# Attention values of two heads side by side in the array's columns, with the weights divided by their sums before they are turned

## The reference, cut to what matters

```python
s = jnp.einsum('bqkgd,bskd->bkgqs', q, k).astype(jnp.float32) * (HEAD_DIM ** -0.5)
p = jax.nn.softmax(s, axis=-1).astype(v.dtype)
return jnp.einsum('bkgqs,bskd->bqkgd', p, v)
```

## Time and profile before

| | us |
|---|---|
| median of three runs | 1839.14 (1838.22 to 1839.6) |
| the profiled execution, its own time | 1839.81 |
| its span, first to last instruction | 1838.0 |
| PE busy | 1762.8 (96%) |
| DVE busy | 1237.6 (67%) |
| ACT busy | 848.0 (46%) |
| POOL busy | 591.6 (32%) |

### The profile page before, as it was taken

How to read it: one execution, slowest core, us unless ns; L and a number is a source line. 1 busy time by engine, 2 the same in 40 slices (tenths; PEclk the granted TensorE clock), 3 DMA queues, 4 the chain that set the end, 5 groups by cost and what they waited for, 6 DMA issues and landing times.

```text
span 1838.0 us, 27537 instructions
## 1 busy us (share of the span) xinstructions
PE 1762.8 (96%) x10200; PEld 1519.2 (83%) x10200; DVE 1237.6 (67%) x2073; ACT 848.0 (46%) x1336; POOL 591.6 (32%) x360
## 2 busy tenths in 40 slices
PE   7978979999999999999999999999999999999998
PEld 7877878777787888888888887888788899989987
DVE  7889765654669587966788885247535665557873
ACT  6654444545224444334444442345453455546654
POOL 4344424211112212321233323224222243525554
PEclk9989999999999999999999999999999999989999
DMA  8545533241224344542345555324222353535553
GB/s 316 211 149 183 183 115 108 65 150 47 58 72 150 105 161 146 175 155 81 126 138 194 184 184 194 87 76 123 85 69 73 94 174 119 171 92 170 182 195 120
DMA packets 71978, 251.80 MB, mean 137 GB/s; under 512 B 7984, under 2 KB 12336, under 8 KB 71216
## 3 DMA queue, kind: packets, MB, share of 16 engines
q1 hardware_dynamic: 66384, 241.74, 40.0%
q10 hardware_dynamic: 5472, 8.39, 1.4%
HBM read 249.05 MB, written 1.05 MB: 136 GB/s over the span
## 4 chain that ended last, share of the span: by engine, by line
PE 67%; DVE 22%; ACT 6%; issue 4%; DMA 1%; ACTq 0%; POOL 0%; DVEq 0%; POOLq 0%
PE bank L643 50%; DVE w_lo L1642 6%; PE bank L774 4%; PE bank L952 4%; DVE mod_w L1697 3%; DVE conv L2509 3%; PE bank L940 2%; PE bank L931 2%; PE bank L1035 2%; DVE probT L1697 1%; ACT w_hi L1122 1%; PE bank L736 1%; PE bank L1024 1%; DVE conv L2516 1%; DVE fT_lo L2518 1%
## 5 line engine op out<-in xcount | busy, mean ns | idle before, releaser
L597 POOL TENSOR_TENSOR w_lo<-w_raw,w_hi 128x512 fp32r<-128x512 f32 x356 | 591.4, 1674 | 1232.2 <-ACT w_hi L1122 1185.0
L1642 DVE TENSOR_TENSOR w_lo<-w_raw,w_hi 128x512 fp32r<-128x512 f32 x356 | 359.2, 1024 | 291.7 <-ACT w_hi L1122 290.7
L1122 ACT ACTIVATE w_hi<-w_raw 128x1024 fp32r<-128x1024 f32 x356 | 367.7, 1053 | 315.3 <-PE bank L643 263.8
L643 PE MATMUL bank<-hT_hi,w_hi 128*128 128x512 f32 (+1 forms) x1280 | 449.6, 351 | 9.7 <-ACT w_hi L1122 3.6
L643 PE MATMUL bank<-hT_hi,w_lo 128*128 128x512 f32 (+1 forms) x1280 | 439.4, 343 | 0.0
L643 PE MATMUL bank<-hT_lo,w_hi 128*128 128x512 f32 (+1 forms) x1280 | 438.9, 343 | 0.0
L643 PEld LDWEIGHTS bank<-hT_hi,w_hi 128*128 128x128 f32 x1280 | 244.5, 191 | 43.9 <-issue 8.0
L643 PEld LDWEIGHTS bank<-hT_hi,w_lo 128*128 128x128 f32 x1280 | 244.0, 191 | 28.3
L643 PEld LDWEIGHTS bank<-hT_lo,w_hi 128*128 128x128 f32 x1280 | 244.5, 191 | 26.9 <-issue 1.0
L1697 DVE SCALAR_TENSOR_TENSOR mod_w<-mod_w,c_rows 128x1024 f32<-128x1024 f32 x96 | 136.6, 1423 | 1.1 <-DMA mod_w<-in_mod_weights 1.1
L643 PE MATMUL bank<-w_hi,hT_hi 128*128 128x512 f32 x272 | 115.5, 425 | 1.9 <-DVE gkT_lo L2219 1.4
(11 more groups left out here) (361 smaller groups left out, 3149.4 us busy)
## 6 DMA issues: line engine op xcount, KB each, us to landing
w_raw<-in_weights SPq DMA_DIRECT2D x356, 512.0 KB, 4.0
mod_w<-in_mod_weights SPq DMA_DIRECT2D x96, 512.0 KB, 3.9
nbias<-in_window_bias ACTq DMA_DIRECT2D x32, 128.0 KB, 2.7
resid_c<-in_ctx ACTq DMA_DIRECT2D x2, 1024.0 KB, 6.4
c_rows<-in_conditions SPq DMA_DIRECT2D x1, 1024.0 KB, 5.7
gatew<-in_gate_weights SPq DMA_DIRECT2D x1, 1024.0 KB, 12.1
decay<-in_decay SPq DMA_DIRECT2D x1, 1024.0 KB, 5.8
out<-resid_x ACTq DMA_DIRECT2D x2, 512.0 KB, 2.6
```

Of the source, the lines that this page charges most:

```text
L597: nc.gpsimd.tensor_tensor(w_lo[:, s, 0, :], w_raw[:, s, 0:COLS], w_hi[:, s, 0, :].bitcast(F32), ALU.subtract).then_inc(lo0_ready, 1)
L643: mm = pe.matmul(held[key][:, oc], st, mv_, start=(opens and k == 0 and t == 0 and i == 0), stop=(closes and k == tiles - 1 and t == 2), s ...
L1122: a.activation(w_hi[:, p % RING].rearrange("p k n -> p (k n)"), w_raw[:, p % RING, :], ACT.Copy).then_inc(hi_ready, 1)
L1642: v.tensor_tensor(w_lo[:, p % RING, 1, :], w_raw[:, p % RING, COLS:KP * COLS], w_hi[:, p % RING, 1, :].bitcast(F32), ALU.subtract).then_in ...
```

## The change

`a_out` takes two heads at once. The values become stationary (128 keys by 64 columns of one head), the turned weights move (128 queries), and the head decides which half of the array's columns and of PSUM's partitions is used. The result comes out with the head dimension on partitions, so that `a_result` goes away and ACT copies bank 7 straight to `y`. The row sums can no longer be applied at the end (queries now lie in the free dimension): DVE multiplies each unit's weights by the reciprocal of its sum in place, between the exponential and the transposes (`scale`, in odd steps, for the pair of the step before). A tile takes eight steps instead of nine, and `prob` has four slots by head. In a step PE now does: scores, then the values of the pair of step s-4, then the transposes of unit s-2.

```diff
     def prob_of(h, t):
-        return (t * AH + h) % 3
-
-    TILE = AH + 1
+        return h % 4
@@ PE
                     def a_turn(h, t):
-                        pe.wait_ge(*exp_done.at((kind, l, h, t)))
+                        pe.wait_ge(*scaled.at((kind, l, h, t)))
...
                     def a_out(h, t):
 
-                        pe.wait_ge(*drained_at((kind, "t", l, h, t)))
+
+                        pe.wait_ge(*drained_at((kind, "t", l, h + 1, t)))
                         if h == 0:
                             take(pe, (kind, "o", l, t), "out")
                         ps = psum((kind, "o", l, t))
                         n = keys(t) // P
-                        g = h // 4 if kind == "ga" else h
                         for j in range(n):
-                            mm = pe.matmul(ps[:, h * HD:(h + 1) * HD], probT[:, h % 2, j * P:(j + 1) * P],
-                                           v_[:, j, g * HD:(g + 1) * HD], start=(j == 0), stop=(j == n - 1))
-                        if h == AH - 1:
+                            for i in range(2):
+                                g = h // 4 if kind == "ga" else h + i
+                                mm = pe.matmul(ps[i * HD:(i + 1) * HD, h // 2 * P:(h // 2 + 1) * P], v_[:, j, g * HD:(g + 1) * HD],
+                                               probT[:, i, j * P:(j + 1) * P], start=(j == 0), stop=(j == n - 1),
+                                               skip_group_check=True)
+                        if h == AH - 2:
                             mm.then_inc(*filled((kind, "o", l, t)))
...
-                    def a_result(t):
-                        pe.wait_ge(*drained_at((kind, "o", l, t)))
-                        ps = take(pe, (kind, "y", l, t), "out")
-                        for j in range(4):
-                            mm = pe.transpose(ps[:, j * P:(j + 1) * P], prob[:, 3, j * P:(j + 1) * P], ident)
-                        mm.then_inc(*filled((kind, "y", l, t)))
-
-                    for s in range(len(q_tts) * TILE + 3):
...
+                    for s in steps_of(q_tts):
+                        if pair(s, q_tts):
+                            a_scores(*pair(s, q_tts))
+                        if pair(s - 4, q_tts):
+                            a_out(*pair(s - 4, q_tts))
                         if unit(s - 2, q_tts):
                             a_turn(*unit(s - 2, q_tts))
@@ ACT
-                        if h >= 3:
-
-                            act.wait_ge(*filled_at((kind, "t", l, h - 3, t)))
+                        if h >= 4:
+                            act.wait_ge(*filled_at((kind, "t", l, h - 4, t)))
...
                     def turned(h, t):
                         if h >= 2:
-                            act.wait_ge(*probT_used.at((kind, l, h - 2, t)))
+                            act.wait_ge(*probT_used.at((kind, l, h // 2 * 2 - 2, t)))
@@ DVE
-                    def divide(t):
...
+                    def scale(h, t):
+
+
+                        dve.wait_ge(*exp_done.at((kind, l, h + 1, t)))
+                        c = 32 + t % 2 * AH + h
+                        v.reciprocal(rs[:, c:c + 2], ss[:, c:c + 2]).then_inc(*W.next())
                         dve.wait_ge(*W.last())
-                        dve.wait_ge(*filled_at(key))
...
+                        for i in range(2):
+                            p_ = prob[:, prob_of(h + i, t), 0:keys(t)]
+                            v.tensor_scalar(p_, p_, rs[:, c + i:c + i + 1], None, ALU.mult)                                .then_inc(*W.tell(scaled, (kind, l, h + i, t)))
...
+                        if pair(s - 1, q_tts):
+                            scale(*pair(s - 1, q_tts))
                         yield
```

More of the change, by code:

```diff
@@ L325, in prob_of, with pair, steps_of @@
     def prob_of(h, t):
-        return (t * AH + h) % 3
-    TILE = AH + 1
+        return h % 4
     def unit(s, tts):
[L333 to L340, removed]
+        i, h = divmod(s, AH)
+        return (h, tts[i]) if s >= 0 and i < len(tts) else None
+    def pair(s, tts):
+        u = unit(s, tts)
+        return u if u and u[0] % 2 == 0 else None
+    def steps_of(tts):
+        return range(len(tts) * AH + 3)
     def V(name, i=0, n=1):
@@ L434, in build @@
     square_ready = Counter("square_ready")
+    scaled = Counter("scaled")
     swapped = Counter("swapped")
@@ L461, in build @@
                lru_ix, lru_mult, lru_y, merged_hi, merged_ready, merged_sum, ml_e, ml_exp, ml_root, ml_ss, ml_w_ready,
-               ml_y, c_ready, neg_max, post_ms, post_root, probT_used, qk_hi, square_ready, swapped, taps_begun, q_ready,
+               ml_y, c_ready, neg_max, post_ms, post_root, probT_used, qk_hi, square_ready, scaled, swapped, taps_begun, q_ready,
                qk_root, qk_ss, resid_ready, ret_hi, ret_root, ret_var, ret_y, root_ready, rows_ready, xT_hi_ready,
@@ L1432, in result @@
                             .then_inc(*A.drain(key))
-                    for s in range(len(q_tts) * TILE + 3):
+                    for s in steps_of(q_tts):
                         if unit(s - 2, q_tts):
                             turned(*unit(s - 2, q_tts))
[L1437 to L1440, removed]
+                        if pair(s - 4, q_tts) and pair(s - 4, q_tts)[0] == AH - 2:
+                            result(pair(s - 4, q_tts)[1])
+                        if pair(s, q_tts):
+                            h, t = pair(s, q_tts)
                             exponential(h, t)
@@ L2175, in maxes @@
                             .then_inc(*W.tell(neg_max, (kind, l, h, t)))
-                    def divide(t):
[L2180 to L2184, removed]
-                        dve.wait_ge(*W.last())
-                        dve.wait_ge(*filled_at(key))
[L2187 to L2195, removed]
+                    def scale(h, t):
+                        dve.wait_ge(*exp_done.at((kind, l, h + 1, t)))
+                        c = 32 + t % 2 * AH + h
+                        v.reciprocal(rs[:, c:c + 2], ss[:, c:c + 2]).then_inc(*W.next())
+                        dve.wait_ge(*W.last())
+                        for i in range(2):
+                            p_ = prob[:, prob_of(h + i, t), 0:keys(t)]
+                            v.tensor_scalar(p_, p_, rs[:, c + i:c + i + 1], None, ALU.mult)                                .then_inc(*W.tell(scaled, (kind, l, h + i, t)))
+                    for s in steps_of(q_tts):
+                        if pair(s, q_tts):
+                            h, t = pair(s, q_tts)
                             maxes(h, t)
                             maxes(h + 1, t)
-                        if tile_end(s - 3, q_tts) is not None:
-                            divide(tile_end(s - 3, q_tts))
+                        if pair(s - 1, q_tts):
+                            scale(*pair(s - 1, q_tts))
                         yield
```

12 lines of the change are left out of this document (3 added, 9 removed).

## The result

The changed kernel takes 1827.96 us (median of four executions, 1822.04 to 1828.88) against 1839.05 (1838.22 to 1839.6) for the kernel before: a ratio of 0.9933, 95% interval 0.9911 to 0.9955. A second set of executions beside the experiments gave 0.9927 (0.9914 to 0.9941). The change makes the kernel about 0.7% faster, 12 to 13 us. Forecast were 34.7 us and a time of 1804.5, with a range up to 1826: the direction is right, the size a third of what was said, and the time is 2 us above the range.

What follows compares the result with a forecast made beforehand. PE was taken to set the pace inside the attentions. Terms: -31.1 (`a_out`) - 5.3 (`a_result`) - 3.3 (end of layer 1's `na`) + 5 (DVE waits) = -34.7 us, giving span 1803.3 and time 1804.5, range 1795 to 1826.

Steps and rivals of the forecast that it cites:

- the column halves work together: In the new `a_out`, instructions go two at a time: 640 x 0.112/2 = 35.8 us instead of 71.7.
- nothing overlaps: Rival on `a_out`: halves do not overlap or a 64-column load costs as much as 128; 1840.3 us, chance 0.09.
- loads stand bare: Rival on `a_out`: 64-column loads do not hide, each instruction costs 0.163 us; 1873 us in all, chance 0.02.
- the old `a_out` was bound by its loads: On PE, old `a_out` cost 0.112 us per instruction for its load, so moving 128 columns instead of 64 is free.
- the size of the saving on PE: `a_out` saves 31.1 us, `a_result`'s transposes 5.3, and the end of layer 1's `na` 3.3.
- the shape change: Values between scores and transposes on PE change the array's shape once more: 0.10 us per pair, 4.8 for 48 pairs.
- the wait of 1.8 at the end: At the end of layer 1's `na`, PE's wait for `divide` before the last `a_result` goes: 1.8 us saved.
- the half clock at the end: After the last `a_result` of layer 1's `na`, PE's stretch at half clock vanishes: 1.5 us saved.
- Cover is missing in three places ... 5 us.: DVE's scaling makes PE wait 2 us at `ga`'s start, 2 in layer 0's `na`, 1 at layer 1's gate rows.
- the half-covered scaling: Rival: in layer 0's 32 pairs each waits most of 1.1 us for DVE, about +20 us; 1819.5 us, chance 0.08.
- A: Experiments' theory: the scaling's place in DVE's queue makes it late, in `na` above all, costing some 23 us of waits.
- B: Experiments' theory: ACT is late, its copy of turned weights standing behind the pair's values and the exponentials behind that copy.

Runs made afterwards that it cites:

- the later version without scaling: Changed kernel with transposes and values one step later in both attentions, and no reciprocal or scaling: 1807.17 us, ratio 0.9821 to the kernel before.
- the later step: Changed kernel with transposes and values one step later: in both attentions 1815.73 us, ratio 0.9862; in `na` alone 1814.43 us, ratio 0.9853.

## Why the prediction was wrong, step by step

**Right: the column halves work together.** Forecast 0.056 us per instruction; measured 0.055, and 0.109 where one half works alone. The rivals in which nothing overlaps (1840.3) and in which loads stand bare (1873) are out. With the latter goes the rule of the Trainium skill on row groups that the prediction weighed (TensorE: Matmul & The Clock Gate, Part 3, The mechanism): both halves use the same rows here and their loads still don't add to the time. The Trainium skill (TensorEngine Tiling (Array Packing), Theoretical Speedup) gives a speedup of up to 2 where a small dimension is at most 64. The traces agree for the 64 columns here: 0.109 us where one half works alone, 0.055 with both. One step on the way is not borne out: that the old `a_out` was bound by its loads. The instructions of one half alone load 64 columns and move 128, and stand as far apart as the old ones, which load 128 and move 64; the rate doesn't tell which of the two it comes from.

**Nearly right: the size of the saving on PE.** (The 1804.5 is the median of before less 34.7; from the stated span of 1803.3 and the 1.8 us that the time lies above it, it would be 1805.1. Nothing hangs on it.) `a_out` was to save 31.1 us. By the rows it is 1.78 - 1.07 = 0.71 for a full pair, 32 of them 23 us, and about 0.26 for each of the 16 pairs with half the keys, 4 us. So 27. The missing 4 us are the shape change: 1.07 less 16 x 0.055 leaves 0.19 per pair where I took 0.10 with 0.16 as the upper end; 48 x 0.09 = 4.3. `a_result` is gone, 5.3, and so is the wait of 1.8 at the end. In sum 34 us of the 38.2 forecast without the clock. The runs confirm the order of it: with the scaling left out and the dates loosened, 33 us are gained by the ratio (0.9821), 26 by the product.

**Wrong: the half clock at the end.** The 1.5 us at half clock behind the last `a_result` were to vanish. They didn't; around the wait of 3.7 us before 1526.88 lies another such stretch, a little earlier and longer (granted clock 0.83 over 1520 to 1540, where 1550 to 1570 had 0.91 before), and the stage has 0.95 in place of 0.98.

**Wrong, and the reason for the miss: "Cover is missing in three places ... 5 us."** The waits are 18.8 us by the trace. The runs put them at 20 by the ratios (33.0 of gain in the later version without scaling, 13.4 in the kernel as it is) and at 11 by the products. With the trace's number the sum comes out: 34 saved less 18.8 is 15, the gain by the product, and 12 to 13 by the ratio, since the changed kernel's clock is a little lower. Three faults are in that step.

- I took the cover from one ordinary step of `ga` and then looked only for stretches where DVE is full. In that step the sum was good: 1.8 us left forecast, 1.9 measured at 394.45. But layer 1's `na` was costed at nothing and has 8.1 us of the waits; the 2 us for layer 0's `na` are 6.7. In layer 1's `na` DVE is far from full (43 of 70 us), and the largest single wait stands there, behind the merge. A share doesn't show what stands ahead of one instruction in the queue. The prediction named that very merge, as the thing that delayed `divide` in the kernel before, and did not ask whether `scale` would stand behind it.
- I asked only who waits for the scaling. 10.1 of the 18.8 us are at lines that were not on the list: the scores, for banks that the exponentials free, and the values, for the copies. The change itself leaves less time for these dates (5.73 instead of 6.5 us per pair of steps, and the copy behind the values), with or without scaling: 10.7 us of such waits stand there when it is left out.
- I took a wait for its own length. Between the version without scaling and the changed kernel lie 16 us by the ratio and 6 by the product; up to 10 of the 16 go with the clock, of which the prediction had no term at all on the side of losses.

In the list of rivals the half-covered scaling came nearest in time (1819.5, by 20 us of waits, where 18.8 are seen), but it placed them in layer 0 at every transpose; they are in both layers, and half of them are at other lines. That its number is near is luck.

**What the theories are worth now.** A holds in layer 1. B in its first form fell. What fits all twelve runs, though no run tests it as a whole, is one chain: scores, maxima (DVE), exponentials (ACT), scaling (DVE), transposes, copy (ACT), values, with three engines that take their parts in a fixed order. Moving one link inside the same number of steps (exponentials first, scaling at once) moves the wait to another line, at the same time or worse; only a step more makes it shorter. Shown: the later step gains 9 to 13 us (product and ratio), in `na`. Not settled: why the profiled executions of some versions have a stretch at half clock behind layer 1's `na`, and others not. That idle time of PE causes such stretches was not tried by itself; I only saw the one follow the other.

## What to carry to other kernels

When an operation is put into the middle of a chain that runs over several engines, write down the dates of the whole chain, in each stage in which it runs, and for each new instruction what stands ahead of it in its engine's queue there; the busy share of the engine doesn't tell. Saving time on the engine that bounds shortens the period of everything around it, so every buffer's release (here the scores' banks) has to be dated again, and if some of them get tight, a step more of distance is cheaper than another order. And when small changes are compared, look at the granted clock of each execution beside its time, and give what you get with it and without.

## What the runs showed of the hardware that I had not expected

- Two column halves work together without strict alternation, but only over a short reach of the instruction order. Four instructions of one half followed by four of the other overlap as well as alternating ones (0.60 against 0.58 us for the eight); of eight and eight the first four and the last four go alone at 0.109 us each, and the mean is 0.087 instead of 0.055.
- The scatter between executions of one kernel goes for the most part with the clock, but not in full: the kernel before had 1835.27 us at a mean granted clock of 0.992 and 1842.95 at 0.987, and at 0.987 there is also one of 1839.79.
